# Merging the two 256-column products of a high weight into one of 512 columns

## The reference

```python
def swiglu(h, w1, w3, w2):
    return (jax.nn.silu(h @ w1) * (h @ w3)) @ w2

for l in range(DEPTH):          # DEPTH = 2
    x   = ffn_sublayer(x,   ..., ffa_w1[l], ffa_w3[l], ffa_w2[l], ...)
    ctx = ffn_sublayer(ctx, ..., ffa_w1[l], ffa_w3[l], ffa_w2[l], ...)
    # rq, rk, rv, rg, nq, nk, nv, fu, gt = split(h @ w_in)
    y_x, y_c = token_mixer(modulate(x, ...), modulate(ctx, ...), mix_w_in[l], ...)
    x = layer_norm(ALPHA * x + g_x * y_x, ...)
    x = ffn_sublayer(x, ..., ffb_w1[l], ffb_w3[l], ffb_w2[l], ...)
    # ctx likewise, in all but the last layer
```

## Time and profile before

| | us |
|---|---|
| median of 3 runs | 2403.34 (2402.38 to 2404.53) |
| the profiled execution, its own time | 2405.37 |
| its span, first to last instruction | 2403.6 |

### The profile page before, as it was taken

How to read it: one execution, slowest core, us unless ns; L and a number is a source line. 1 busy time by engine, 2 the same in 40 slices (tenths; PEclk the granted TensorE clock), 3 DMA queues, 4 the chain that set the end, 5 groups by cost and what they waited for, 6 DMA issues and landing times.

```text
span 2403.6 us, 33104 instructions
## 1 busy us (share of the span) xinstructions
PE 2358.5 (98%) x13276; PEld 2040.5 (85%) x13276; DVE 1614.8 (67%) x2135; ACT 939.3 (39%) x1389; POOL 126.4 (5%) x158
## 2 busy tenths in 40 slices
PE   7999999999999999999999999999999999999998
PEld 4988988998877888898889888889889896997996
DVE  7667658856378545686766786766688556778656
ACT  3422355442126322353224464224455323544443
POOL 1000001101100000010000010000010010000000
PEclk9999999999999999999999999999999999999999
DMA  8655565651233444544556575456556243675763
GB/s 288 182 168 171 193 193 167 182 178 64 54 111 85 126 132 126 163 133 157 170 169 198 177 221 161 158 171 201 187 179 189 94 134 103 214 253 189 230 202 123
DMA packets 466444, 396.33 MB, mean 165 GB/s; under 512 B 34148, under 2 KB 418292, under 8 KB 466036
## 3 DMA queue, kind: packets, MB, share of 16 engines
q1 hardware_dynamic: 450704, 386.98, 51.2%
q10 hardware_dynamic: 15588, 7.23, 1.1%
HBM read 392.99 MB, written 1.17 MB: 164 GB/s over the span
## 4 chain that ended last, share of the span: by engine, by line
PE 88%; DVE 7%; DMA 1%; issue 1%; ACT 1%; ACTq 0%; POOL 0%; SPq 0%; DVEq 0%
PE ps L1631 26%; PE ps L1633 26%; PE ps L1632 26%; DVE wl L1014 2%; PE ps L1928 1%; PE ps L2004 1%; PE ps L1983 1%; PE ps L2097 1%; DMA raw<-in_ada_w 1%; DVE st L1082 1%; ACT wh L587 1%; PE ps L1678 1%; PE ps L1909 1%; PE ps L1738 1%; PE ps L1992 1%
## 5 line engine op out<-in xcount | busy, mean ns | idle before, releaser
L1014 DVE TENSOR_TENSOR wl<-raw,wh 128x1024 fp32r<-128x1024 f32 x560 | 681.7, 1221 | 565.5 <-ACT wh L587 564.2
L587 ACT ACTIVATE wh<-raw 128x1024 fp32r<-128x1024 f32 x560 | 591.9, 1059 | 1182.8 <-PE ps L1633 1096.9
L1631 PE MATMUL ps<-hh,wh 128*128 128x256 f32 (+1 forms) x2720 | 887.0, 326 | 2.6 <-DVE kq L1516 1.5
L1632 PE MATMUL ps<-hl,wh 128*128 128x256 f32 (+1 forms) x2720 | 880.9, 324 | 0.0
L1633 PE MATMUL ps<-hh,wl 128*128 128x256 f32 (+1 forms) x2720 | 880.7, 324 | 0.0
L1631 PEld LDWEIGHTS ps<-hh,wh 128*128 128x128 f32 x2720 | 518.3, 191 | 46.6 <-DVE kq L1516 3.1
L1633 PEld LDWEIGHTS ps<-hh,wl 128*128 128x128 f32 x2720 | 518.2, 191 | 41.0
L1632 PEld LDWEIGHTS ps<-hl,wh 128*128 128x128 f32 x2720 | 518.4, 191 | 40.8
L1029 DVE SCALAR_TENSOR_TENSOR acc<-araw,c,acc 128x1024 f32<-128x1024 f32 x210 | 258.6, 1280 | 59.7 <-DMA araw<-in_ada_w 58.2
L1631 PE MATMUL ps<-wh,stage_h_f 128*128 128x512 f32 x616 | 240.7, 391 | 2.0 <-DVE stage_l_f L1271 2.0
L1632 PE MATMUL ps<-wl,stage_h_f 128*128 128x512 f32 x616 | 239.8, 389 | 0.0
(11 more groups left out here) (202 smaller groups left out, 2314.7 us busy)
## 6 DMA issues: line engine op xcount, KB each, us to landing
raw<-in_ffa_w SPq DMA_DIRECT2D x204, 512.0 KB, 4.0
raw<-in_ffb_w SPq DMA_DIRECT2D x168, 512.0 KB, 4.2
raw<-in_mix_w_in SPq DMA_DIRECT2D x148, 512.0 KB, 4.2
araw<-in_ada_w SPq DMA_DIRECT2D x136, 512.0 KB, 5.2
raw<-in_ret_w_out SPq DMA_DIRECT2D x16, 512.0 KB, 4.3
raw<-in_na_fou_w_out SPq DMA_DIRECT2D x16, 512.0 KB, 4.0
raw<-in_mix_w_o SPq DMA_DIRECT2D x16, 512.0 KB, 3.9
raw<-in_ada_w SPq DMA_DIRECT2D x8, 512.0 KB, 5.6
```

Of the source, the lines that this page charges most:

```text
L587: A.activation(w_home(u)[0], raw[:, s, :], ACT.Copy).then_inc(w_rounded, 1)
L1014: V.tensor_tensor(low, raw[:, s, :], f(high), ALU.subtract).then_inc(w_split, 1)
L1631: T.matmul(out, a[0], b[0], start=start, stop=False)
L1632: T.matmul(out, a[0], b[1], start=False, stop=False)
```

## The change

`hh` and `hl` become the two halves of one tensor, so that `wh` can be multiplied with both in one matmul of 512 columns. The product with `hh` then stands in columns 0 to 255 of the bank, that with `hl` in 256 to 511. `wl*hh` is added in 0 to 255. A unit has 8 matmuls of 512 columns and 8 of 256. The halves of the bank are added afterwards: ACT copies the second to SBUF, DVE adds the first. It applies to units of 256 columns where `paired` says so: all steps of the heads of FFN 0 and FFN 5 (which has nothing else), the tails of FFN 0, 2 and 3, and all of `ret_in`. That is 100 FFN units (FFN 0: 14 in the head and 14 in the tail, FFN 2 and 3: 14 each, FFN 5: 44) and 32 + 20 of `ret_in`, 152 in all. The heads of FFN 2 and 3 stay as they were.

```diff
-        hh = sb("hh", [P, KD, TOK], F32R)
-        hl = sb("hl", [P, KD, TOK], F32R)
+        hhl = sb("hhl", [P, 2, KD, TOK], F32R)
+        hh, hl = hhl[:, 0], hhl[:, 1]
...
+        def paired(i, q):
+            p, lo, hi = ffn_steps(i)[q]
+            return hi - lo == SEQ and (i in (0, SUBS - 1) or lo == SEQ)
... ACT, FFN step
+                    if paired(i, q):
+                        A.copy(sgf[:, j, SEQ:TOK], ps[:, B[2 * j], SEQ:TOK]).then_inc(ff_half, 1)
+                        act.wait_ge(ff_sum, 2 * pair0(i, q) + 1)
+                        A.activation(sgf[:, j, 0:SEQ], sgf[:, j, SEQ:TOK], ACT.Sigmoid).then_inc(ff_sig, 1)
+                    else:
+                        A.activation(sgf[:, j, lo:hi], ps[:, B[2 * j], lo:hi], ACT.Sigmoid).then_inc(ff_sig, 1)
...
                     rounded(v + 5)
+                    if paired(i, q):
+                        act.wait_ge(unit_done, v + 2)
+                        act.wait_ge(ff_gate, m + q + 1)
+                        A.copy(sgf[:, j, SEQ:TOK], ps[:, B[2 * j + 1], SEQ:TOK]).then_inc(ff_half, 1)
... ACT, ret_in
                     rounded(u + 4 + j)
+                    act.wait_ge(unit_done, u + j + 1)
+                    A.copy(rgz[:, r, lo:hi] if r < KD else kq[:, r - KD, lo:hi], ps[:, in_bank(l, j), SEQ:TOK]).then_inc(in_half, 1)
... DVE, FFN step
                     split(v + 4)
+                    if both_halves:
+                        dve.wait_ge(ff_half, 2 * pair0(i, q) + 1)
+                        V.tensor_tensor(half, half, ps[:, B[2 * j], 0:SEQ], ALU.add).then_inc(ff_sum, 1)
                     dve.wait_ge(ff_sig, m + q + 1)
-                    V.tensor_tensor(sgb, sgb, ps[:, B[2 * j], lo:hi], ALU.mult).then_inc(ff_gate, 1)
+                    V.tensor_tensor(sgb, sgb, half if both_halves else ps[:, B[2 * j], lo:hi], ALU.mult).then_inc(ff_gate, 1)
                     split(v + 5)
                     dve.wait_ge(ff_gate, m + q + 1)
+                    if both_halves:
+                        dve.wait_ge(ff_half, 2 * pair0(i, q) + 2)
+                        V.tensor_tensor(half, half, ps[:, B[2 * j + 1], 0:SEQ], ALU.add).then_inc(ff_sum, 1)
+                        dve.wait_ge(ff_sum, 2 * pair0(i, q) + 2)
... DVE, ret_in
-                    dve.wait_ge(unit_done, u + n + 1)
-                    V.tensor_copy(dst, ps[:, bank, lo:hi]).then_inc(in_copied, 1)
+                    dve.wait_ge(in_half, sum(RET[:l]) + n + 1)
+                    V.tensor_tensor(dst, dst, ps[:, bank, 0:SEQ], ALU.add).then_inc(in_copied, 1)
... PE
+            def form_pair(u, bank, n0):
+                s = u % RING
+                ready(u)
+                for kt in range(KD):
+                    c = kt * P
+                    if kt:
+                        T.matmul(ps[:, bank, 0:SEQ], wl[:, s, c:c + P], hh[:, kt, n0:n0 + SEQ], start=False, stop=False)
+                    ins = T.matmul(ps[:, bank, :], wh[:, s, c:c + P], hhl[:, :, kt, n0:n0 + SEQ], start=kt == 0, stop=kt == KD - 1)
+                    if kt == 0:
+                        T.matmul(ps[:, bank, 0:SEQ], wl[:, s, c:c + P], hh[:, kt, n0:n0 + SEQ], start=False, stop=False)
+                ins.then_inc(unit_done, 1)
```

More of the change, by code:

```diff
@@ L242, in trunk @@
         ff_sig, ff_gate, ff_mul = sem("ff_sig"), sem("ff_gate"), sem("ff_mul")
+        ff_half, ff_sum, in_half = sem("ff_half"), sem("ff_sum"), sem("in_half")
         stage_hi, stage_lo = sem("stage_hi"), sem("stage_lo")
@@ L357, in ff0, with pair0 @@
             return sum(len(ffn_steps(j)) for j in ffns if j < i)
+        def paired(i, q):
+            p, lo, hi = ffn_steps(i)[q]
+            return hi - lo == SEQ and (i in (0, SUBS - 1) or lo == SEQ)
+        def pair0(i, q):
+            return sum(paired(j, k) for j in ffns for k in range(len(ffn_steps(j))) if (j, k) < (i, q))
         def half_step(i, p, half):
@@ L370, in trunk, with in_bank @@
         X_UNITS = 16
+        def in_bank(l, n):
+            m = [slot[1] if slot[0] == "unit" else None for slot in ret_slots(l)].index(n)
+            return in_banks(3 * l + 1)[m % 4]
         r_items = [[(h, s) for h in range(RH) for s in range(2 if l < DEPTH - 1 else 1)] for l in range(DEPTH)]
@@ L717, in ffn @@
                     act.wait_ge(ff_mul, m + q + 1)
-                    A.activation(sgf[:, j, lo:hi], ps[:, B[2 * j], lo:hi], ACT.Sigmoid).then_inc(ff_sig, 1)
+                    if paired(i, q):
[4 more added lines that the diff above has]
+                        A.activation(sgf[:, j, lo:hi], ps[:, B[2 * j], lo:hi], ACT.Sigmoid).then_inc(ff_sig, 1)
                     if htiles(i) == NT and q in (3, 5):
@@ L813, in mixer @@
                 u = AT["ret_in", l]
-                for j in range(RET[l]):
+                for j, (r, lo, hi) in enumerate(ret_steps(l)):
                     rounded(u + 4 + j)
+                    act.wait_ge(unit_done, u + j + 1)
+                    A.copy(rgz[:, r, lo:hi] if r < KD else kq[:, r - KD, lo:hi], ps[:, in_bank(l, j), SEQ:TOK]).then_inc(in_half, 1)
                     if j == 6:
@@ L1314, in ffn @@
                     v, j = u + 2 * q, q % 2
-                    sgb = sgf[:, j, lo:hi]
+                    both_halves, half = paired(i, q), sgf[:, j, SEQ:TOK]
+                    sgb = sgf[:, j, 0:SEQ] if both_halves else sgf[:, j, lo:hi]
                     if i == 0 and q == HEAD + 8 + DEPTH:
@@ L1334, in ffn @@
                     split(v + 4)
+                    if both_halves:
+                        dve.wait_ge(ff_half, 2 * pair0(i, q) + 1)
+                        V.tensor_tensor(half, half, ps[:, B[2 * j], 0:SEQ], ALU.add).then_inc(ff_sum, 1)
                     dve.wait_ge(ff_sig, m + q + 1)
-                    V.tensor_tensor(sgb, sgb, ps[:, B[2 * j], lo:hi], ALU.mult).then_inc(ff_gate, 1)
+                    V.tensor_tensor(sgb, sgb, half if both_halves else ps[:, B[2 * j], lo:hi], ALU.mult).then_inc(ff_gate, 1)
                     split(v + 5)
                     dve.wait_ge(ff_gate, m + q + 1)
-                    dve.wait_ge(unit_done, v + 2)
-                    V.tensor_tensor(g[:, p, lo:hi], sgb, ps[:, B[2 * j + 1], lo:hi], ALU.mult).then_inc(ff_mul, 1)
+                    if both_halves:
+                        dve.wait_ge(ff_half, 2 * pair0(i, q) + 2)
+                        V.tensor_tensor(half, half, ps[:, B[2 * j + 1], 0:SEQ], ALU.add).then_inc(ff_sum, 1)
+                        dve.wait_ge(ff_sum, 2 * pair0(i, q) + 2)
+                    else:
+                        dve.wait_ge(unit_done, v + 2)
+                    V.tensor_tensor(g[:, p, lo:hi], sgb, half if both_halves else ps[:, B[2 * j + 1], lo:hi], ALU.mult).then_inc(ff_mul, 1)
                     if q == gate_step:
@@ L1655, in form_a, with ffn_unit, edge_unit @@
                     ins.then_inc(unit_done, 1)
-            def edge_unit(i, u, bank, n):
+            def form_pair(u, bank, n0):
[9 more added lines that the diff above has]
+                ins.then_inc(unit_done, 1)
+            def ffn_unit(i, q, u, bank):
+                p, lo, hi = ffn_steps(i)[q]
+                if paired(i, q):
+                    form_pair(u, bank, lo)
+                else:
+                    form_a(u, bank, (hh, hl), hi, n0=lo)
+            def edge_unit(i, u, bank):
                 s = u % RING
@@ L1661, in edge_unit @@
                 pe.wait_ge(k_lo, edge_halves(i, LT - 1))
-                for kt in range(KD):
+                for kt in range(KD - 1):
                     if kt == K_HALF:
                         pe.wait_ge(h_lo, pre0(i) + LT)
-                    w = wh[:, s, kt * P:(kt + 1) * P]
-                    T.matmul(ps[:, bank, 0:n], w, hh[:, kt, 0:n], start=kt == 0, stop=False)
-                    T.matmul(ps[:, bank, 0:n], w, hl[:, kt, 0:n], start=False, stop=False)
+                    T.matmul(ps[:, bank, :], wh[:, s, kt * P:(kt + 1) * P], hhl[:, :, kt, 0:SEQ], start=kt == 0, stop=False)
                 ready(u)
                 for kt in range(KD):
-                    ins = T.matmul(ps[:, bank, 0:n], wl[:, s, kt * P:(kt + 1) * P], hh[:, kt, 0:n], start=False, stop=kt == KD - 1)
-                ins.then_inc(unit_done, 1)
+                    T.matmul(ps[:, bank, 0:SEQ], wl[:, s, kt * P:(kt + 1) * P], hh[:, kt, 0:SEQ], start=False, stop=False)
+                T.matmul(ps[:, bank, :], wh[:, s, (KD - 1) * P:KD * P], hhl[:, :, KD - 1, 0:SEQ], start=False, stop=True).then_inc(unit_done, 1)
             def first(u):
@@ L1845, in ffn @@
                     if q == 0 and i in EDGE:
-                        edge_unit(i, v, B[2 * j], hi)
+                        edge_unit(i, v, B[2 * j])
                     else:
-                        form_a(v, B[2 * j], src, hi, n0=lo)
+                        ffn_unit(i, q, v, B[2 * j])
                     if htiles(i) == NT and q in (3, 5):
@@ L1860, in ffn @@
                         ada_turns(i, 1)
-                    form_a(v + 1, B[2 * j + 1], src, hi, n0=lo)
```

(3 more changed lines are left out.)

## The result

| | before | after |
|---|---|---|
| median (5 runs each, same chip) | 2403.79 us (2402.38 to 2404.71) | 2413.02 us (2411.08 to 2415.43) |
| ratio after / before | | 1.0037 [1.0026, 1.0048] |
| profiled execution: time / span | 2405.37 / 2403.6 | 2412.16 / 2410.4 |

What follows compares the result with a forecast made beforehand. PE was taken as the bound, busy 98% of the span; 8.3 - 4.5 - 2.1 + 3.8 + 1.7 = +7.2 us on a median of 2403.3 gave 2410.5, range 2399 to 2416.

Steps and rivals of the forecast that it cites:

- late transposes in FFN 0: FFN 0's head: PE waits 3.0 and 2.7 us at tiles 2 and 3, normalised later by ACT.
- a late gate in FFN 5: FFN 5: PE's gate products start at 2265.8 instead of 2259.3, 6.5 us late, 5.4 of it one wait.
- FFN 0, head: Head of FFN 0: ACT's and DVE's queue order delays PE; loss 8.3 us, the gain of 14 units included.
- tails: Tails of FFN 0, 2 and 3: DVE's 5.25 us step stays under PE's 5.55; gain 42 x 0.107 = 4.5 us.
- ret_in: `ret_in`: some units' savings lost to waits; gain 2.1 us, from 1.7 in layer 0 and 0.4 in layer 1.
- FFN 5 with clock: FFN 5: 6.12 us `ada` steps delay the gate, loss 3.8 us; 1.7 more for lower clock behind its wait.
- Gain on PE: All 152 merged units: each 0.107 us shorter, taking the merged matmul at 0.2267; at most 16.2 us.
- third rival: All merged units: the merged matmul takes 0.240 us and saves nothing on PE; 2419.8 us, chance 0.07.
- the bank of step 1: FFN 0's head: PE wants this bank at 60.5 and gets it at 61.89, after DVE's product.
- the late `modulate` of tile 3: `ret_in`, layer 0: `modulate` comes one copy (0.3 us) later, so units 13 to 15 gain nothing and earlier savings go.
- Clock: Behind FFN 5's wait of 5.4 us: lower clock costs 1.7, from 0 to 1.7; FFN 0's possible 1 taken as 0.

Runs made afterwards that it cites:

- norm_early: Against the changed kernel, in FFN 0 ACT normalises tiles 2 and 3 at steps 2 and 4, right behind the rounding there; 2411.68 us, ratio 1.0034.
- no_adds: Changed kernel without ACT's copies and DVE's adds, first half of the bank read directly, so the product with `hl` is left out; 2391.56 us, ratio 0.9948.
- accl_early: Changed kernel with FFN 0's head unmerged, FFN 5's gate products at step 14 instead of 9, and its `acch` and `accl` one step earlier; 2398.62 us, ratio 0.9983.
- head0_off: Changed kernel with FFN 0's head back on the old 256-column units, all else still merged; 2404.99 us, ratio 1.0004.
- gate_late: Changed kernel with FFN 5's gate products in step 14 instead of 9; 2409.99 us, ratio 1.0024.
- head0_off_gate_late: Changed kernel with FFN 0's head back on old units and FFN 5's gate products in step 14 instead of 9; 2401.35 us, ratio 0.9994.
- tails_only: Changed kernel with FFN 0's head and FFN 5 back on old units; the three tails and `ret_in` stay merged; 2398.2 us, ratio 0.9976.
- accl_early_late_pairs: Changed kernel, FFN 0's head and FFN 5 before step 10 unmerged, FFN 5's `acch` and `accl` a step earlier, gate at step 10; 2395.28 us, ratio 0.9965.

## Why the prediction came out

The sign and the size were right, and the two mechanisms that cost (late transposes in FFN 0, a late gate in FFN 5) are the ones measured. That the sum is as close as 0.1 is partly luck: two terms are off by 1.2 and 1.1 in opposite directions, and FFN 0's head agrees only with 1.7 us of lower clock in it that I had taken as 0.

| term | forecast | measured |
|---|---|---|
| FFN 0, head | +8.3 | +8.3 |
| tails | -4.5 | -3.3 |
| `ret_in` | -2.1 | -3.2 |
| FFN 5 with clock | +3.8 + 1.7 | +5.3 |
| sum | +7.2 | +7.1 (span +6.8, medians +9.2) |

- **Gain on PE.** The mechanism holds, the size was off: a unit saves 0.083, not 0.107, because I took the merged matmul at its lower bound, 0.2267, when it costs 0.230. Over 42 units that is 3.5; measured is 1.12 in each of the three FFNs, 3.3 to 3.4 together, which accounts for the tails within 0.2. The third rival, 0.240, is out.
- **FFN 0, head.** The order of ACT and DVE, written out instruction by instruction, held. Forecast: the bank of step 1 at 61.89, waits at the transposes of 3.0 and 2.7, the first wide unit at 93.95 against 85.6. Measured: 61.12, 2.60 and 2.3, 93.04 against 85.30 (the stage itself began 0.45 earlier in the kernel after). What I would not say again is that the normalisation's place is the cause: `norm_early` took both waits away and gained 0.55. The list of waits names what came last, and behind it the next thing was as late.
- **Tails.** No waits, as forecast: a step without extra work is under PE's two units.
- **`ret_in`.** Layer 0 was forecast 1.7 and measured 2.1, layer 1 0.4 and 1.1. The wait on `kq` rose from 1.5 to 2.4, as the late `modulate` of tile 3 said. For layer 1 I let only units 16 to 19 count, and 20 units at 0.083 are 1.7, of which 1.1 came; which of the others gained was not looked into.
- **FFN 5.** DVE's step of 6.12 with an `ada` was measured as 6.11, PE's gate products at 2266.29 for 2265.8, the wait as 5.2 for 5.4. The listed waits on `g` were 0.24 each, not 0.5: a step is 6.11 - 5.59 = 0.52 longer than two units, and part of that stands elsewhere, 0.10 of it in the first matmul behind the wait (0.50 long for 0.40). By the stages: 44 units save 3.5 (`no_adds` 125.62 for 129.09). `no_adds` less its wait of 1.3 at the gate is 124.3, and `accl_early`, with no such wait, takes 128.63: 4.3 given back in steps paced by DVE, about eight times 0.52. The kernel after has the gate's wait and the lower clock on top: 128.6 + 5.2 + 2.2 = 136.0, measured 134.97, and 135.78 in `head0_off`. The account is good to about 1 us.
- **What I had wrong in it** was the cause of the gate's wait. I put all of it down to lag. The two kernels with the late gate showed that 2.8 of it is `accl`'s place behind the product of the step before, and would be there without any lag. The size came out because I followed the instructions' order and not the story told beside it.
- **Clock.** 1.7 was taken from a spell of 3.4 at the lower level. Around the wait of 5.2 the spell was 6.8, and PE worked in 4.4 of it: 2.2, above my bound of 1.7 (in `head0_off` in 5.1 of it: 2.6). What I expected of `gate_late` took 4.6 and 2.3. In FFN 0 one spell of 3.4 followed the waits (window 82 to 87, granted clock 0.66: 1.7), where I took 0; it is inside the +8.3, so the rest of the head was that much better than followed.

## What to carry to other kernels

When an operation is handed from a full engine to idle ones, don't ask how busy these are but write their in-order lists out, one step long, with the durations of the rows: a dependence that goes across and back (ACT, DVE, ACT) holds everything behind it on both engines, and here 0.36 + 0.41 a unit on engines 41% and 69% busy cost some 21 us (the kernel after against `no_adds`). Use such a trade only in steps whose list is shorter than PE's, which here made a loss of 0.4% a gain of 0.35%. A wait in the list shows who came last and not what a repair is worth; look at what is late behind it, and move one engine's place against the other's, not both together.

## What the runs showed of the hardware

- A matmul of 512 columns whose moving operand lies in two runs of 256 takes 0.230 us from start to start, against 0.2267 for one run and 2 x 0.120 for two matmuls. The Trainium skill, "TensorE: Matmul & The Clock Gate", section "Back-to-back issue gap", puts 2.5 ns over the columns' time for what it calls the isolated gap, and says that in a stream with weight loads the spacing is another. The rows here, which have a weight load for each matmul, show 13 ns over it for the plain one and some 17 for the one in two runs.
- The sigmoid of 256 columns takes longer from SBUF than from PSUM, and the add is as long as the product was. Groups by shape, after, beside the earlier trace rows (364 and 414):

```profile
L736 ACT ACTIVATE sgf<-sgf 128x256 f32<-128x256 f32 x50 | 20.9, 418 | 100.4 <-DVE sgf L1364 100.4
...
L1371 DVE TENSOR_TENSOR sgf<-sgf,ps 128x256 f32<-128x256 f32 x50 | 20.7, 414 | 0.0
...
L734 ACT COPY sgf<-ps 128x256 f32<-128x256 f32 x50 | 17.7, 354 | 0.0
```

  ACT idles 100.4 us in all ahead of the sigmoid, for DVE's add; in the tails PE waits for none of it, in FFN 0's head the waits of PE go back to it.
- A longer wait of PE doesn't fix the length of the spell at 1.2 GHz that comes with it. The wait of 5.2 us came with 6.8 us in all three kernels that have it (after, `head0_off`, `norm_early`). But the same wait of 2.83 came with 6.8 in `gate_late` and with 3.4 in `head0_off_gate_late`, and in layer 1's mixer `tails_only`, `no_adds` and `accl_early_late_pairs` have 6.8 (from 2032 or 2035 on) behind waits of at most 1.5 each, where the kernel before has 3.4 (from 2043 on). Such a spell moves a whole time by up to 1.7 us or so without any change in the code, which is to be kept in mind for the differences of 1 us between kernels here.
